# Three groups of transfers begun a stage earlier: the recurrence's first chunk, the first attention's first pair, the output weights' second half

## The chip, the cores and the metric

The kernel runs on one core of a Trainium2 chip. A core has a matrix engine (PE, its weight loads PEld), a vector engine (DVE), a scalar engine (ACT), GpSimd (POOL) and SyncE (SP), which here only issues transfers. All engines run their own instruction streams and meet through semaphores. All data is float32; the on-chip memory is one array named `arena` of 128 partitions by 53208 words. The metric is the device time of one execution in microseconds (us), median of three runs: 4931.64 us before the change (4931.13 to 4935.05).

## What is computed

Two blocks in a row, on 1024 tokens of width 1024. The first block:

```python
h = rmsnorm(x, g_mix_pre);  proj = h @ w_in
out_a = gated_deltanet(...)          # chunked delta rule, 4 heads of 128
out_b = dilated_attention(...)       # 8 heads of 64, with a bias table
x = x + rmsnorm(concat(out_a, out_b) @ w_out, g_mix_post)
x = x + rmsnorm((silu(h2 @ w_gate) * (h2 @ w_up)) @ w_down, g_ffn_post)
```

The second block has two layers, over the 1024 tokens and 256 context tokens:

```python
u = (x * (1 + scale) + shift) @ w_in
y_r = rwkv7_bidirectional(u)         # 6 heads of 64, forward and backward recurrence
y_a = grouped_query_attention(u)     # 6 query heads
y_n = neighbourhood_attention(u)     # 4 heads
x = layer_norm(ALPHA * x + gate * (concat(y_r * silu, y_a * silu, y_n * silu) @ w_out))
```

## The kernel before

The program is a list of stages. A stage has one generator per engine; `Stage.drive` steps the main stage's generator and those of the stages that run `beside` it (on another "lane", with semaphores of its own). At the end of a stage PE, ACT, DVE and POOL each count up `stage_end` (`arrive`) and wait until all four have (`leave`, the value `meet`). SP takes no part in that meeting: `emit` runs only the main stages' `sp` in order, so SP runs ahead until a wait that is written into `sp` stops it. Whatever stands behind such a wait in SP's stream waits too.

The order of the main stages is: token norm; `PairProj` (the projections of block 1, with the preparation of the delta rule beside it); `Gdn` (the delta rule); `Attention` (dilated, four pairs of heads, eight query tiles each); `TokenPairs` (product with `w_out`, with `TokenRows`, the normalization, beside it); `GatedPairs` and a second `TokenPairs` (the gated network); then for each of two layers `PairProj` (with `NaBand`, `RwkvPrep` and `GqaPrep` beside it, in this order), `Rwkv` (the recurrence, ten chunks), `Attention` `gqa` (three pairs, with `RwkvOut` beside it), `Attention` `na` (two pairs), and `TokenPairs`.

The matrix products of `PairProj` and `TokenPairs` use seven half-size products in place of eight (P1, P5, P6, P7, P2, P3, P4 in the order of issue, `ORDER`). Their operands are sums: T1 = B12 - B11, T2 = B22 - T1, T4 = B21 - T2, T3 = B22 - B12 for the right side, S1 to S4 for the left. DVE makes them at the start of `TokenPairs`, in the order S1, T1, S2, T2, T4, S4, T3, S3 (`right_sum` at L1086, `left_sum` at L1062). P1 needs B11, P5 needs T1, P6 needs T2 and P7 needs S3. B11 and B12 are rows 0 to 3 of the weights (transfers j = 0 to 3), B21 and B22 rows 4 to 7.

The waits of SP that matter here:

- `PairProj.sp` (L369): the stores of a unit's blocks at n = 5, 6, 7 (L380), before them the store of the context columns at n = 1 (L413). POOL waits at the end of the stage until all stores have landed (L595).
- `Rwkv.sp` (L3128): waits for `self.meet - 4`, the end of the stage ahead, then issues the ten transfers of chunk 0 (L3135), then the first two pairs of `gqa` (`next_loads`, L2385), then those of chunk 1. PE waits for the K, B, V and Q parts before its first product (L3218). On POOL the stage begins with two clears (L3163) and the table of decay factors `fc` (L3169 to L3172, 18 small products); the first thing DVE does with a product of PE is behind a wait for that table (L3386), and its result (L3394) is what POOL continues with (L3178, L3182).
- The first `Attention`: `first_loads` (L2387) waits for `gdn.meet` and then issues pair 0 (five transfers) and pair 1.
- `TokenPairs.sp` (L968): the dictionary `after` gives the stage's end to wait for ahead of transfer j. Block 1 has `{0: gdn.meet}`, so all eight rows of `w_out` are fetched during the attention. The layers of block 2 have `{0: gqa.meet, 4: na.meet}`: rows 4 to 7 wait for the end of `na`, because their place in `arena` (columns 4096 to 8191) holds the masks of `na`.

```python
dve.drain().then_inc(s.sem, 1)                # Rwkv.run_dve, L3385
dve.wait_ge(O.sem, O.at(0, "fc"))
for n in range(NCH + 1):
```

Of the kernel before, what the change touches and what calls it, by code (L numbers as in the profile page):

```python
# [12 lines left out]
P = 128  # L13
TOP = 53208
D = 1024
# [182 lines left out]
class Stage:  # L198
# [16 lines left out]
    def sp(self, sp): pass  # L215
# [47 lines left out]
class PairProj(Stage):  # L263
# [9 lines left out]
    def __init__(self, core, w, tiles, x, first, out, room, eighth=(), silu=(), late=(), keep=False):  # L273
# [58 lines left out]
        self.steps = (3 if self.alone else 0) + 8 * self.N  # L332
# [36 lines left out]
    def sp(self, sp):  # L369
# [33 lines left out]
        for u in range(self.N):  # L403
            for n in range(8):
                if n in (5, 6, 7):
                    store(u, ("22", "11", "12")[n - 5])
# [460 lines left out]
class TokenPairs(Stage):  # L867
# [6 lines left out]
    def __init__(self, core, room, w, lhs, first, n, sums=None, spare=None, after=()):  # L874
# [13 lines left out]
        if not sums:  # L888
            W = core.W.rearrange("p (k f) -> p k f", k=8)
            self.B = {f"B{i + 1}{j + 1}": W[:, 4 * i:4 * i + 4, 512 * j:512 * j + 512] for i in range(2) for j in range(2)}  # L890
# [77 lines left out]
    def sp(self, sp):  # L968
        E, C = self.s_pe, len(self.cuts)
        for j in range(self.chunks):  # L970
            if j in self.after:
                sp.wait_ge(self.c.stage_end.sem, self.after[j])
# [17 lines left out]
            else:  # L990
                sp.dma_start(self.c.W[:, j * D:j * D + D], self.w[j]).then_inc(self.c.w_in[j].sem, 16)
# [1284 lines left out]
class Attention(Stage):  # L2276
# [9 lines left out]
    def __init__(self, core, room, pairs, n_q, n_k, units, loads, out, bias=None, extra=(), pool_bias=None, once=(), gate=None,  # L2286
                 home=None, pair_room=None, extra_room=None, sems=(0, 1, 2), start=((), ()), ahead=False):
# [7 lines left out]
        pair = lambda *shape: (pair_room or room).take(core, *shape)  # L2295
# [8 lines left out]
        self.extra = [(extra_room or room).take(core, 2, n) for n in extra]  # L2304
# [18 lines left out]
        self.steps = self.N + 2  # L2323

# [718 lines left out]
def tri(a):  # L3043
    return a.rearrange("p (h t) -> p h t", h=3)
# [10 lines left out]
class Rwkv(Stage):  # L3055
# [4 lines left out]
    def __init__(self, core, rw, fac, y, areas):  # L3060
        super().__init__(core)
        self.rw, self.fac, self.y = rw, fac, y
# [14 lines left out]
        self.fc = core.region(areas[-1][1], NCH, 2 * RT)  # L3077
# [49 lines left out]

    def sp(self, sp):  # L3128
        E, A = self.s_pe, self.s_act

        def load(n, part, i):
            for d, c in ((0, n), (1, self.back(n))):
                for x in part:
                    src = self.rw[x + str(d) if x != "V" else "V"].rearrange("(j p) t -> p j t", p=P)[:, :, c * P:(c + 1) * P]
                    sp.dma_start(tri(self.b[f"{x}{d}{n % 2}"]), src).then_inc(self.c.w_in[3 * (n % 2) + i].sem, 16)  # L3135

        sp.wait_ge(self.c.stage_end.sem, self.meet - 4)
        load(0, "KBV", 0)
        load(0, "Q", 1)
        load(0, "R", 2)  # L3140
        self.next_loads(sp)
        for n in range(NCH + 1):
            if n + 1 < NCH:
                if n > 0:
                    sp.wait_ge(E.sem, E.at(0, f"tB1@{n - 1}"))
                load(n + 1, "KBV", 0)
                if n > 0:
                    sp.wait_ge(E.sem, E.at(0, f"G1@{n}"))
                load(n + 1, "Q", 1)
                if n > 0:  # L3150
                    sp.wait_ge(E.sem, E.at(0, f"O1@{n}"))
                load(n + 1, "R", 2)
# [604 lines left out]
def second_block(nc, core, a, p2, fac, ms, gate_rows, h, h_at, x_home):  # L3757
# [12 lines left out]
    for l in range(2):  # L3770
# [13 lines left out]
        rwkv = Rwkv(core, rw, fac, y_dir, [(h_at, h_at + KT * TOK2), (big, top - 64)])  # L3784
# [274 lines left out]
```

## Time and profile before

| | |
|---|---|
| median of three runs | 4931.64 us |
| the profiled execution | 4922.9 us, span 4921.1 us |
| mean granted clock of PE | 0.966 |
| PE busy | 4553.9 us (93%) |
| PEld busy | 2888.5 us (59%) |
| DVE busy | 2715.9 us (55%) |
| ACT busy | 1465.5 us (30%) |
| POOL busy | 975.7 us (20%) |

PE is busy nearly throughout, and matmuls are pipelined with modelled ends, so a busy PE isn't PE at its peak. The idle time that is left stands mainly at the seams of the stages. Every row of the trace begins with a start time counted from the span's start, so two rows of one stretch can be subtracted. "Releaser" is what ended an engine's idle time.

### The profile page before, as it was taken

To read this page: it belongs to the slowest core of one execution; us is meant where nothing else is said; L and a number is where in the kernel's file an instruction comes from. 1 tells how busy PE (TensorE), PEld (TensorE's weight loads), DVE (VectorE), ACT (ScalarE), POOL (GpSimd) and SP (SyncE) were. 2 spreads that over 40 slices of the span, in tenths; PEclk is the share of its full clock that TensorE was granted. 3 is DMA by queue.
4 is the path that set the end of the run, shared out by engine and by line. 5 is a ranking of instruction groups with operands and counts; after the bars stand their busy time and mean duration, and the time that the engine had idled before them with its cause. 6 is when DMAs were issued, how large, how long until landed. Compare 5 with 4: busy or idle time off the path is not lost. (4 is left out here: it accounts for less than half of the span.)

```text
span 4921.1 us, 96946 instructions
## 1 busy us (share of the span) xinstructions
PE 4553.9 (93%) x41054; PEld 2888.5 (59%) x41054; DVE 2715.9 (55%) x4643; ACT 1465.5 (30%) x2452; POOL 975.7 (20%) x1174
## 2 busy tenths in 40 slices
PE   7998978899999989998999888998999799989897
PEld 4445955444444445554999755654544499976563
DVE  3763457786432336765545466566686445436556
ACT  1222353200000113332223255533342133236552
POOL 0002311000100000001233233620000132324460
PEclk9999999999999999999999999999999899989998
DMA  2332022343424544444221112113444411111222
GB/s 91 112 98 74 2 82 82 124 135 114 162 94 160 177 134 150 143 162 134 64 61 55 46 45 56 50 61 120 150 146 163 138 55 55 54 32 52 72 56 76
DMA packets 344923, 471.84 MB, mean 96 GB/s; under 512 B 39799, under 2 KB 247959, under 8 KB 343536
## 3 DMA queue, kind: packets, MB, share of 16 engines
q1 hardware_dynamic: 292416, 267.83, 17.5%
q0 software_dynamic: 52080, 197.81, 11.5%
q8 instruction: 330, 5.41, 0.5%
q14 instruction: 97, 0.79, 0.1%
HBM read 330.50 MB, written 148.65 MB: 97 GB/s over the span
## 5 line engine op out<-in xcount | busy, mean ns | idle before, releaser
L471 PE MATMUL psum<-arena 128*128 128x512 f32 x2352 | 1035.4, 597 | 12.2 <-POOLq L222 6.5
L3212 PE MATMUL psum<-arena 64*64 64x64 f32 (+5 forms) x23040 | 905.1, 232 | 34.7 <-DMA arena<-rw_Q 23.9
L3212 PEld LDWEIGHTS psum<-arena 64*64 64x64 f32 (+3 forms) x23040 | 866.0, 144 | 75.7 <-issue 47.3
L471 PEld LDWEIGHTS psum<-arena 128*128 128x128 f32 x2352 | 448.1, 191 | 561.4 <-issue 542.1
L1028 PE MATMUL psum<-arena 128*128 128x512 f32 x1344 | 589.1, 599 | 21.8 <-DVE arena L1086 11.4
L686 PE MATMUL psum<-arena 128*128 128x512 f32 x1232 | 535.7, 595 | 6.2 <-DVE arena L752 2.7
L2585 DVE CUSTOM_DVE_ANT_0 arena<-psum,arena 128x512 f32<-128x512 f32 (+3 forms) x532 | 292.8, 588 | 326.3 <-PE psum L2472 309.1
L1028 PEld LDWEIGHTS psum<-arena 128*128 128x128 f32 x1344 | 257.0, 192 | 344.2 <-issue 321.3
L686 PEld LDWEIGHTS psum<-arena 128*128 128x128 f32 x1232 | 232.3, 190 | 302.9 <-issue 290.9
L2472 PE MATMUL psum<-arena 64*128 64x512 f32 (+3 forms) x1192 | 275.4, 548 | 105.3 <-DVE arena L2585 70.0
L3416 DVE TENSOR_TENSOR arena<-arena,psum 128x384 f32<-128x384 f32 x320 | 177.9, 556 | 330.8 <-PE psum L3212 297.4
L2550 ACT COPY arena<-psum 128x512 f32<-128x512 f32 (+3 forms) x532 | 244.3, 512 | 306.5 <-PE psum L2523 300.6
L2442 POOL TENSOR_TENSOR arena<-arena 128x512 f32<-128x512 f32 (+2 forms) x192 | 221.9, 1166 | 475.5 <-ACT arena L2550 475.3
L2523 PEld LDWEIGHTS psum<-arena 128*128 128x128 f32 x1736 | 186.6, 142 | 151.0 <-issue 118.0
L2556 ACT ACTIVATE arena<-arena 128x1280 f32<-128x1280 f32 (+5 forms) x244 | 256.8, 1066 | 46.2 <-DVEq L2606 46.1
L2523 PE MATMUL psum<-arena 128*128 128x128 f32 x1736 | 251.5, 283 | 10.5 <-ACT arena L2550 9.6
L2488 PE MATMUL psum<-arena 128*64 128x128 f32 x3472 | 251.1, 281 | 8.2 <-DVE arena L2600 8.2
L2488 PEld LDWEIGHTS psum<-arena 128*64 128x64 f32 x3472 | 187.0, 137 | 52.9 <-issue 34.4
L2472 PEld LDWEIGHTS psum<-arena 64*128 64x128 f32 x1192 | 100.5, 196 | 179.6 <-DVE arena L2585 100.8
L3372 ACT COPY arena<-psum 128x384 f32<-128x384 f32 x200 | 96.1, 480 | 321.6 <-PE psum L3212 321.6
L3192 POOL TENSOR_TENSOR arena<-arena 128x384 f32<-128x384 f32 x160 | 155.3, 997 | 171.9 <-PE psum L3212 171.9
L3376 ACT COPY arena<-psum 128x384 f32<-128x384 f32 x240 | 101.7, 496 | 204.2 <-PE psum L3212 203.7
(341 smaller groups left out, 5223.3 us busy)
## 6 DMA issues: line engine op xcount, KB each, us to landing
arena<-w_in SPq DMA_DIRECT2D x86, 512.0 KB, 5.7
proj<-arena SPq DMA_DIRECT2D x172, 256.0 KB, 2.0
arena<-w_mod POOLq DMA_DIRECT2D x24, 1024.0 KB, 5.7
arena<-proj POOLq DMA_DIRECT2D x34, 640.0 KB, 5.1
arena<-down_sum SPq DMA_DIRECT2D x40, 512.0 KB, 3.6
arena<-proj SPq DMA_DIRECT2D x28, 640.0 KB, 7.0
arena<-w_down SPq DMA_DIRECT2D x30, 512.0 KB, 3.6
x_home<-arena POOLq DMA_DIRECT2D x26, 512.0 KB, 4.2
```

The lines of the kernel that those rows point to most:

```text
L471: ins = pe.matmul(ps[:, b, :], L[:, k, :], R[:, k, :], start=(p in ("P1", "P5", "P6", "P7") and k == 0), stop=(k == KT // 2 - 1), skip_gro ...
L686: ins = pe.matmul(self.c.psum[:, b, :], L[:, k, :], R[:, k, :], start=(begins and k == 0), stop=(k == KT // 2 - 1), skip_group_check=True)
L1028: ins = pe.matmul(self.bank(j, b), self.left(p, j, left, *g)[:, k - g[0], :], R[:, k - k0, :], start=(x in ("P1", "P5", "P6", "P7") and k ...
L2442: ins = pool.tensor_tensor(t[:, 0:m], x[:, 0:m], x[:, 512:512 + m], ALU.add)
L2472: ins = pe.matmul(ps[:, j, at:at + m], self.q[HALF[j], self.slot(it), q * P:(q + 1) * P], self.k[HALF[j], self.slot(it), k0:k0 + m], start ...
L2488: pe.matmul(ps[HALF[j], bank, 0:P], self.vT[:, it % 2, tiles[c] * P + 64 * j:tiles[c] * P + 64 * j + 64], self.pt[n % 2][j][:, c * P:(c + ...
L2523: ins = pe.transpose(out[:, x:x + P], self.p[n % 3][j][:, at + x:at + x + P], ident)
L2550: act.copy(self.pt[n % 2][j][:, at:at + w], ps[:, 2 + j, 0:w]).then_inc(A.sem, 1)
L2556: act.activation(self.p[x][g][:, 0:wide], self.p[x][g][:, 0:wide], ACT.Exp, bias=low, scale=-1.0).then_inc(A.sem, 1)
L2585: dve.tensor_tensor_reduce(self.p[x][j][:, at:at + w], ps[:, j, 0:w], add, -1.0, 3e38, ALU.add, ALU.min, self.acc[:, 2 * x + j, g:g + 1]). ...
L3212: return pe.matmul(out, lhsT, rhs, start=first, stop=last, skip_group_check=not (first and last))
L3416: dve.tensor_tensor(dst, dst, ps, ALU.subtract).then_inc(s.sem, 1)
```

## The change

- `PairProj.sp` calls `next_loads` in its last unit, at n = 4, ahead of that unit's block stores. In block 2 that is the new `Rwkv.first_loads`: SP waits for the end of `RwkvPrep` (`prep.meet`) and issues chunk 0's ten transfers there. `Rwkv.sp` begins with `gqa`'s pairs instead. Chunk 0's ten buffers move to the top of the arena.
- The first `Attention` keeps the buffers of its pairs in two places far apart (`pair_at`): slot 0 in columns 2048 to 7167, which `Gdn` doesn't use, slot 1 in the old area. Pair 0 is fetched once `gemm.meet` has come, which is ahead of `Gdn`; pair 1 after `gdn.meet` as before.
- As slot 0 now lies where `w_out` goes, `TokenPairs` of block 1 fetches rows 0 and 1 after `gdn.meet` and rows 2 to 7 only after the last output of the attention's pair 2 (`out{3 * att.per - 1}`, counted by DVE).
- `TokenPairs` of block 2 has its rows 4 to 7 in the slot of `gqa`'s and `na`'s pair buffers that is free after `na`'s pair 0 (`low`), and fetches them after that pair's last output (`out{na.per - 1}`).

```diff
@@ PairProj
-        self.steps = (3 if self.alone else 0) + 8 * self.N
+        self.steps, self.next_loads = (3 if self.alone else 0) + 8 * self.N, lambda sp: None
...
         for u in range(self.N):
             for n in range(8):
+                if n == 4 and u == self.N - 1:
+                    self.next_loads(sp)
@@ TokenPairs
-    def __init__(self, core, room, w, lhs, first, n, sums=None, spare=None, after=()):
+    def __init__(self, core, room, w, lhs, first, n, sums=None, spare=None, low=None, after=()):
...
-            self.B = {f"B{i + 1}{j + 1}": W[:, 4 * i:4 * i + 4, 512 * j:512 * j + 512] for i in range(2) for j in range(2)}
+            W = [W[:, 0:4, :], W[:, 4:8, :] if low is None else low]
+            self.resident = [W[k // 4][:, k % 4, :] for k in range(8)]
+            self.B = {f"B{i + 1}{j + 1}": W[i][:, :, 512 * j:512 * j + 512] for i in range(2) for j in range(2)}
...
-                sp.wait_ge(self.c.stage_end.sem, self.after[j])
+                sp.wait_ge(*self.after[j])
...
-                sp.dma_start(self.c.W[:, j * D:j * D + D], self.w[j]).then_inc(self.c.w_in[j].sem, 16)
+                sp.dma_start(self.resident[j], self.w[j]).then_inc(self.c.w_in[j].sem, 16)
@@ Attention
-        pair = lambda *shape: (pair_room or room).take(core, *shape)
+        self.pair_at = pair_at and list(pair_at)
+        pair = lambda *shape: self.apart(*shape) if pair_at else (pair_room or room).take(core, *shape)
...
+    def apart(self, _, n):
+        at, far = self.pair_at
+        self.pair_at[0] += n
+        return self.c.arena[:, at:at + 2 * far].rearrange("p (a b) -> p a b", a=2)[:, :, 0:n]
@@ Rwkv
-        self.fc = core.region(areas[-1][1], NCH, 2 * RT)
+        self.fc = core.region(areas[0][1], NCH, 2 * RT)
...
+    def first_loads(self, sp):
+        sp.wait_ge(*self.ready)
+        for i, part in enumerate(("KBV", "Q", "R")):
+            self.load(sp, 0, part, i)
+
     def sp(self, sp):
         E, A = self.s_pe, self.s_act
...
         sp.wait_ge(self.c.stage_end.sem, self.meet - 4)
-        load(0, "KBV", 0)
-        load(0, "Q", 1)
-        load(0, "R", 2)
         self.next_loads(sp)
@@ second_block
-        rwkv = Rwkv(core, rw, fac, y_dir, [(h_at, h_at + KT * TOK2), (big, top - 64)])
+        rwkv = Rwkv(core, rw, fac, y_dir, [(top - 64 - 10 * 384, top - 64), (h_at, h_at + KT * TOK2), (big, top - 64 - 10 * 384)],
+                    (side.stage_end.sem, prep.meet))
+        gemm.next_loads = rwkv.first_loads
...
-                          after={0: gqa.meet, 4: na.meet})
+                          low=R(x_at, 4, 2 * TOK2)[:, :, TOK2:TOK2 + D],
+                          after={0: (core.stage_end.sem, gqa.meet), 4: (na.s_dve.sem, na.s_dve.at(0, f"out{na.per - 1}"))})
@@ program
-        room = Room((big, TOP))
+        room = Room((big + 5 * SEQ, TOP))
...
-                        sems=core.w_in[0:3], start=([(core.stage_end.sem, gdn.meet)], ()),
+                        sems=core.w_in[0:3], start=([(core.stage_end.sem, gemm.meet)], [(core.stage_end.sem, gdn.meet)]),
+                        pair_at=(2048, big - 2048),
...
-        prod = TokenPairs(core, room, [token(a["w_out"], k) for k in range(KT)], mixT, 0, SEQ // P, after={0: gdn.meet})
+        prod = TokenPairs(core, room, [token(a["w_out"], k) for k in range(KT)], mixT, 0, SEQ // P, after={0: (core.stage_end.sem, gdn.meet), 2: (att.s_dve.sem, att.s_dve.at(0, f"out{3 * att.per - 1}"))})
```

## Rows read from the trace of the kernel before

**Rows 1.** Who waited, PE alone: engine, line, releaser: us, times, longest.

```profile
PE psum L3212 <- DMA arena<-rw_Q: 23.9, 2, 12.0
...
PE psum L2472 <- DMA arena<-bias_band: 13.0, 1, 13.0
...
PE psum L1028 <- DVE arena L1086: 11.4, 2, 6.6
```

**Rows 2.** The chain that ended last: start us, us, what; last stage.

```profile
4790.61 9.96 DMA arena<-w_out
```

**Rows 3.** Timeline, delta rule to attention: start us, us, instruction [idle before].

```profile
620.30 0.10 POOL L2411 MEMSET arena<- 128x1 f32 x1 [15.49 <-ACTq L222]
...
632.55 0.80 PE L2472 MATMUL psum<-arena 64*128 64x128 f32 x4 [12.97 <-DMA arena<-bias_band]
...
635.34 3.04 PE L2240 MATMUL psum<-arena 128*128 128x512 f32 x4
```

**Rows 4.** Windows of 2 us: busy by engine, PEclk, DMA share, GB/s.

```profile
634.00:636.00 2.00, 1.82 (x5) 1.03 (x6) 0.59 (x5) 0.69 (x2) 0.00 (x0) 0.50 1.03 414
...
4402.00:4404.00 2.00, 2.00 (x5) 0.47 (x3) 0.00 (x0) 0.00 (x0) 0.00 (x0) 0.50 0.00 0
```

**Rows 5.** Timeline, first layer, projections to recurrence.

```profile
2318.36 0.37 SPq L3135 DMA_DIRECT2D arena<-rw_K  x1
...
2320.31 2.73 POOL L3172 TENSOR_TENSOR arena<-arena 128x3 f32<-128x3 f32 x18
...
2326.53 4.11 PE L3212 MATMUL psum<-arena 64*64 64x64 f32 x120 [11.84 <-DMA arena<-rw_Q]
...
2328.20 1.02 DVE L3394 TENSOR_TENSOR arena<-psum,arena 128x384 f32<-128x384 f32 x2 [8.94 <-PE psum L3212]
```

**Rows 6.** Timeline, second layer, the same place.

```profile
3898.09 2.74 POOL L3172 TENSOR_TENSOR arena<-arena 128x3 f32<-128x3 f32 x18
...
3904.51 3.64 PE L3212 MATMUL psum<-arena 64*64 64x64 f32 x120 [12.04 <-DMA arena<-rw_Q]
...
3906.18 1.02 DVE L3394 TENSOR_TENSOR arena<-psum,arena 128x384 f32<-128x384 f32 x2 [9.13 <-PE psum L3212]
```

**Rows 7.** Timeline, end of the projections: first layer, then one row of the second.

```profile
2174.15 1.07 POOL L3580 DMA_DIRECT2D arena<-proj  x2 [8.38 <-POOLq L222]
...
2283.79 0.80 SPq L413 DMA_DIRECT2D proj<-arena  x2
...
2292.40 3.22 POOL L3604 DMA_DIRECT2D kx<-arena  x6 [24.82 <-DVEq L3694]
...
2300.45 15.97 SPq L380 DMA_DIRECT2D proj<-arena  x4
...
2305.85 8.84 PE L471 MATMUL psum<-arena 128*128 128x512 f32 x16 [3.38 <-POOLq L222]
...
3870.29 3.23 POOL L3604 DMA_DIRECT2D kx<-arena  x6 [24.78 <-DVEq L3694]
```

**Rows 8.** Timeline, start of TokenPairs in block 1.

```profile
821.22 10.58 PE L1028 MATMUL psum<-arena 128*128 128x512 f32 x24 [1.46 <-DVEq L222]
...
832.83 9.68 PE L1028 MATMUL psum<-arena 128*128 128x512 f32 x22 [1.03 <-DVE arena L1062]
...
836.54 0.69 DVE L1092 TENSOR_TENSOR arena<-arena,psum 128x512 f32<-128x512 f32 x1 [0.71 <-PE psum L1028]
```

**Rows 9.** Timeline, start of TokenPairs in the second layer.

```profile
4789.27 7.14 PE L1028 MATMUL psum<-arena 128*128 128x512 f32 x16 [1.91 <-DVEq L222]
...
4800.69 4.62 DVE L1086 TENSOR_TENSOR arena<-arena 128x2048 f32<-128x2048 f32 x2 [7.89 <-DMA arena<-w_out]
...
4812.95 0.69 DVE L1092 TENSOR_TENSOR arena<-arena,psum 128x512 f32<-128x512 f32 x1 [0.48 <-PE psum L1028]
```

**Rows 10.** Timeline, start of TokenPairs in the first layer.

```profile
3245.26 7.87 PE L1028 MATMUL psum<-arena 128*128 128x512 f32 x14
...
3267.47 0.69 DVE L1092 TENSOR_TENSOR arena<-arena,psum 128x512 f32<-128x512 f32 x1 [0.66 <-PE psum L1028]
```

More of the change, by code:

```diff
@@ L2286, in __init__ @@
     def __init__(self, core, room, pairs, n_q, n_k, units, loads, out, bias=None, extra=(), pool_bias=None, once=(), gate=None,
-                 home=None, pair_room=None, extra_room=None, sems=(0, 1, 2), start=((), ()), ahead=False):
+                 home=None, pair_room=None, pair_at=None, extra_room=None, sems=(0, 1, 2), start=((), ()), ahead=False):
         super().__init__(core)
@@ L2303, in __init__ @@
         self.rec, self.acc, self.nm, self.zero = take(2, P), take(6, 4), take(6, 1), take(1)
-        self.extra = [(extra_room or room).take(core, 2, n) for n in extra]
+        self.extra = [pair(2, n) if pair_at else (extra_room or room).take(core, 2, n) for n in extra]
         self.tree = [[take(min(self.width - 512, 512)) for _ in range(2)] for _ in range(2)]
@@ L3055, with __init__ @@
 class Rwkv(Stage):
-    def __init__(self, core, rw, fac, y, areas):
+    def __init__(self, core, rw, fac, y, areas, ready):
         super().__init__(core)
-        self.rw, self.fac, self.y = rw, fac, y
+        self.rw, self.fac, self.y, self.ready = rw, fac, y, ready
         self.nb = 8
@@ L3126, in back, with load @@
         return nctx - 1 - n if n < nctx else NCH + nctx - 1 - n
+    def load(self, sp, n, part, i):
+        for d, c in ((0, n), (1, self.back(n))):
+            for x in part:
+                src = self.rw[x + str(d) if x != "V" else "V"].rearrange("(j p) t -> p j t", p=P)[:, :, c * P:(c + 1) * P]
+                sp.dma_start(tri(self.b[f"{x}{d}{n % 2}"]), src).then_inc(self.c.w_in[3 * (n % 2) + i].sem, 16)
+    def first_loads(self, sp):
+        sp.wait_ge(*self.ready)
+        for i, part in enumerate(("KBV", "Q", "R")):
+            self.load(sp, 0, part, i)
     def sp(self, sp):
         E, A = self.s_pe, self.s_act
[L3131 to L3135, printed above, removed]
         sp.wait_ge(self.c.stage_end.sem, self.meet - 4)
-        load(0, "KBV", 0)
-        load(0, "Q", 1)
-        load(0, "R", 2)
         self.next_loads(sp)
@@ L3145, in sp @@
                     sp.wait_ge(E.sem, E.at(0, f"tB1@{n - 1}"))
-                load(n + 1, "KBV", 0)
+                self.load(sp, n + 1, "KBV", 0)
                 if n > 0:
                     sp.wait_ge(E.sem, E.at(0, f"G1@{n}"))
-                load(n + 1, "Q", 1)
+                self.load(sp, n + 1, "Q", 1)
                 if n > 0:
                     sp.wait_ge(E.sem, E.at(0, f"O1@{n}"))
-                load(n + 1, "R", 2)
+                self.load(sp, n + 1, "R", 2)
             if n > 0:
@@ L3971, in program @@
         room = Room((big + FFT * SEQ, TOP))
-        prod = TokenPairs(core, room, kview(a["w_down"]), act, 0, SEQ // P, sums, h[:, :, TOK2 - 512:TOK2], after={6: ffn.meet})
+        prod = TokenPairs(core, room, kview(a["w_down"]), act, 0, SEQ // P, sums, h[:, :, TOK2 - 512:TOK2], after={6: (core.stage_end.sem, ffn.meet)})
         prod.beside = [TokenRows(core.lanes[1], room, prod, tiles, "rms", {"g": row_of(a["rows"], 1)}, h, extra=extra, slots=1)]
```

## The prediction

> **What bounds the kernel now.** I read the waits of PE first, since PE is busy 93% of the span. Three of its waits are for a transfer that begins only when the stage that needs it begins: 23.9 us in two pieces before the recurrence (one per layer), 13.0 us before the first attention, and 11.4 us in two pieces inside `TokenPairs`, where the row names DVE's sum (L1086) as the releaser [rows 1]. The chain that ended last goes through the third kind: 9.96 us of `w_out` a few microseconds after the last stage opens [rows 2]. Then I read the timeline of each of these five seams, and asked not how long PE waits but what would be late next, since DVE and POOL have start-up work of their own in the same microseconds. In all five the stage order is a barrier for every computing engine, so a microsecond saved at a seam shifts all that follows.
>
> **The change part by part.** Everything is taken from the profiled execution (4922.9 us); the median is 8.7 us above it, and I carry the saving over to the median unchanged.
>
> *First attention.* POOL's first instruction of the stage is at 620.30, PE's first product at 632.55, and PE had been idle for 12.97 us, that is since 619.58 [rows 3]. With pair 0 fetched ahead of the delta rule, PE can start about 0.1 us after the stage opens, at 620.4. DVE and POOL only clear small tiles there (0.10 us). The saving is 632.55 - 620.4 = 12.15 us. Pair 1 still leaves at 620.3; it is needed eight query tiles later. The first tiles are short chains PE, DVE, ACT, and between them PE waits as it did. The clock is the unknown. After the idle 12.97 us PE ran at the granted clock 0.50, the 1.2 GHz level [rows 4], and the product beside the attention took 3.04 us [rows 3]. If the new start, which comes after only 0.8 us of idle, keeps 2.4 GHz, up to half of that and of the small products around it goes, 2 us. Against that, in the second layer's `gqa` start, a sparse start that followed a busy stage with a short gap, the clock stood at 0.50 even 14 us in [rows 4]; if the same happens here for such a time, with PE busy about two thirds of it, it costs some 3 us. I take 0, nearer to neither, and keep -3 to +2. Part: **12.1 us**.
>
> *The recurrence, twice.* PE waits until 2326.53, and SP issues the first transfer at 2318.36, which is when the stage opens [rows 5]. The whole wait would be 8.1 us. But DVE may not touch PE's first product before POOL has made the table of decay factors, and this ends at 2320.31 + 2.73 = 2323.04 [rows 5]. Now DVE's first product is at 2328.20; with the data present it comes at about 2323.1, 5.1 us earlier. From there POOL's and PE's chain (L3178, L3182, PE) follows as now. In the second layer the table ends at 3898.09 + 2.74 = 3900.83 and DVE's product was at 3906.18 [rows 6]: 5.3 us. So PE's wait shrinks by 8 us, but PE gets a new wait of some 3 us a moment later, behind its first 120 products; what ends last is POOL's table. Part: **10.4 us**, bounds 9 (PE at the low clock for longer, since its work there is now broken in two) and 11.7 (DVE no longer waits 0.7 us between its two kinds of first products, as ACT has then long delivered).
>
> *What the moved issue costs.* The ten transfers go ahead of the last unit's block stores on SP's queue. SP has issued the context store at 2283.79 + 0.80 and its next instruction is a block store that could not leave before 2300.45 [rows 7]. Ten issues of about half a microsecond each fit in this hole: no store is later. The wait for `RwkvPrep` ahead of them passes at once: POOL began `GqaPrep`, which comes behind that meeting, at 2174.15 [rows 7]. In the old place the ten transfers took from 2318.36 to 2326.53, 8.2 us in all [rows 5]; from 2284.6 that ends at about 2292.8. POOL's six stores of `kx` leave from 2292.40, and PE waits for their landing (through the end of `GqaPrep`) until 2305.85, 3.38 us [rows 7]. The overlap is under a microsecond. I cost it at nothing. In the second layer `kx` leaves at 3870.29 [rows 7] and the last unit has no context store ahead of the hole, so SP is there earlier still. The first two pairs of `gqa` and chunk 1 leave 5 us earlier than now and are needed tens of microseconds later: nothing.
>
> Here a rule of the Trainium skill speaks against the change (DMA: Bandwidth & Descriptors, "Issuing engines are not separate DMA queues"): transfers issued by SP and by GpSimd run on the same 16 engines and interleave, so an early load isn't free for a store on another queue. By the rule, with the two bursts on top of each other, the stores of `kx` would be late by as much as the loads take; by the rows they nearly miss each other. This is the second rival below.
>
> *TokenPairs in block 2, twice.* Block 1's stage is the pattern, since all its weights are present: it starts at 821.22, three products take 10.58 us, P7 starts at 832.83, 11.6 us after the start, because DVE's sums (S3 is the last) take this long; DVE's sum after P7 is at 836.54, 15.3 us after the start [rows 8]. In the second layer the stage starts at 4789.27, T2 waits 7.89 us for `w_out`, and the sum after P7 is at 4812.95, 23.7 us after the start [rows 9]. With rows 4 to 7 present this stage should run as block 1's: 23.7 - 15.3 = 8.4 us. That is more than the DMA wait, for two reasons: P6 ran at the low clock after the gap, and PE's gap was longer than what DVE lost. In the first layer PE's first two products end at 3245.26 + 7.87 = 3253.13 and the sum after P7 is at 3267.47 [rows 10]. P6 adds a third of 10.58, 3.5 us, so 3256.7; S3 is ready at about 3255.9, so it isn't the limit; P7 and its sum take 836.54 - 832.83 = 3.7 us more [rows 8]: 3260.4, and the saving is 7.1 us. Part: **15.5 us**. The bound from below is PE's gap alone, 11.4 us [rows 1]; from above 16.5, had the first layer its early products at the second's pace. SP's new wait here is for `na`'s pair 0, half a stage before the end; four rows take about 10 us [rows 2], and behind it in SP's queue stand only the next stage's loads, which wait for PE's last product anyway.
>
> *w_out in block 1* now comes after the attention's pair 2, a quarter of the 200 us stage (620.30 to 821.22 [rows 3, 8]) before it is needed: 50 us for six rows, which at the pace of [rows 2] take 15 us. Nothing; without that cover it would cost what block 2's stages lost.
>
> **Sum:** 12.1 + 10.4 + 15.5 = 38.0 us, so 4922.9 becomes 4884.9 in a profiled execution and the median 4931.6 becomes **4893.6**. With all bounds at their ends the saving is 29.5 or 44 us: 4902 or 4887.5.
>
> **The rivals.**
> *The clock takes part of it back.* PE has less idle time at the seams, but the starts stay sparse, and PE stays at 1.2 GHz longer in the attention and in both recurrences. For it: the row at 4402 [rows 4]. Against it: in `TokenPairs` the opposite must happen, as dense products follow on each other. Price 3 us and twice 2 us: 4900 us. Chance 0.15.
> *The loads collide with the stores of `kx`.* If the ten loads push the landing of `kx` by their full 8.2 us, PE's wait of 3.38 us at L471 grows by this in both layers [rows 5, 7]: 16.4 us lost, 4910 us. Against it: the loads start 7.8 us before. Chance 0.06.
> *It doesn't do what it says in the first attention:* PE waits for something else at 620.4, or pair 1 lands too late for tile 8 and the wait comes back there. That gives 12.1 us back: 4906 us. Against it: tile 8 comes over 20 us later. Chance 0.04.
> *Slower than before.* SP now waits for `RwkvPrep` ahead of the last unit's stores, and the stage can't end before these land. One microsecond that `RwkvPrep` ends after 2300.45 is one microsecond that the stage ends later. Below about 19 us per layer the rest of the saving still covers it; from there the kernel is slower, and at 25 us late per layer it would be 4944 us. In the trace `RwkvPrep` ended over 120 us before [rows 7], so the change would have to slow it greatly, which nothing in it does. Chance 0.02.
>
> **How the numbers follow.** The forecast has 0.73: 4893.6, its own range 4888 to 4900. Adding the clock's rival and half of the others' nearer side, and the 1 to 3 us by which medians of this kernel move, the range is 4886 to 4905. A measurement of this kernel can tell about 0.2%, 10 us, from no change; a saving below 10 us needs the collision and another failure together. Faster 0.96, same 0.02, slower 0.02.
>
> **What would show each step.** Right: `rw_Q` and `bias_band` are gone from PE's waits; DVE L3394 comes 4.8 us after the recurrence's stage opens, straight after POOL L3172, and PE shows a new wait for POOL L3182 of 3 to 4 us; the sum after P7 comes 15 to 16 us after each `TokenPairs` starts, and no DMA wait stands at L1086; PE's wait at L471 for POOL's queue stays at 3 to 4 us. Wrong: a wait at L471 of over 5 us (collision); the first 15 us of the attention at the low clock; stores of the last unit issued later than 2300; a wait for `w_out` at the start of block 1's `TokenPairs`.

## The result, and the profile after

In the first series of timings the changed kernel took 4878.42 us (median of four, 4876.26 to 4880.86) and the kernel before 4931.39 us (4928.27 to 4935.05): a ratio of 0.9892, 95% interval 0.9875 to 0.991, a saving of 53 us (by the interval 44 to 62) where 38.0 us was forecast. The forecast said 4893.6 us with a range of 4886 to 4905, so the direction was right and the size wrong. Two further series, taken with the experiments, gave smaller savings:

| series | before, median (runs) | changed, median (runs) | saving | ratio, 95% interval |
|---|---|---|---|---|
| first | 4931.39 (4) | 4878.42 (4) | 53.0 | 0.9892, 0.9875 to 0.991 |
| second | 4926.11 (7) | 4882.45 (4) | 43.7 | 0.9913, 0.9898 to 0.9927 |
| third | 4927.76 (9) | 4880.19 (4) | 47.6 | 0.9902, 0.9886 to 0.9918 |
| all executions | 4927.7 (35) | 4880.9 (13) | 46.8 | |

The 35 executions of the kernel before lie between 4917 and 4939 us (standard deviation 4.9), the 13 of the changed one between 4876 and 4886 (3.1). So there are two questions: what the five openings really gave, and what the rest is.

The head of the changed kernel's page: the span, and the busy time of the engines.

```profile
span 4875.0 us, 96946 instructions
PE 4541.5 (93%) x41054; PEld 2881.5 (59%) x41054; DVE 2716.3 (56%) x4643; ACT 1465.8 (30%) x2452; POOL 976.6 (20%) x1174
```

Who waited on PE, changed kernel (engine, line, releaser: us in total, times, longest):

```profile
PE psum L3226 <- POOL arena L3196: 9.9, 4, 4.4
...
PE psum L3226 <- POOLq L222: 7.7, 2, 4.0
PE psum L473 <- POOLq L222: 7.1, 2, 4.1
...
PE psum L1033 <- DVEq L222: 5.3, 3, 1.9
...
PE psum L1033 <- DVE arena L1067: 3.1, 3, 1.0
```

All three waits of [rows 1] are gone: no transfer of `rw_Q` or `bias_band` releases PE, and in `TokenPairs` DVE's sum costs 3.1 us for three stages, the waits that block 1's stage always had. A new wait stands at the top, PE for POOL's L3196 in the recurrence (L3182 before), as the forecast said.

**First attention.** The timeline of PE, changed kernel (start us, us, instruction, idle before and its releaser), which answers [rows 3], and two windows (length, busy time of PE, PEld, DVE, ACT, POOL, then the granted clock, the share of DMA and GB/s), which answer [rows 4]:

```profile
615.75 0.50 PE L1960 MATMUL psum<-arena 128*128 128x128 f32 x3
616.96 0.49 PE L2484 MATMUL psum<-arena 64*128 64x128 f32 x4 [0.71 <-ACTq L222]
618.30 0.70 PE L2484 MATMUL psum<-arena 64*128 64x256 f32 x4 [0.84 <-DVEq L2618]
618.93 1.98 PE L2245 MATMUL psum<-arena 128*128 128x512 f32 x4
```

```profile
615.00:620.00 5.00, 3.44 (x23) 2.28 (x22) 2.49 (x13) 2.34 (x4) 1.25 (x3) 1.00 0.40 121
620.00:625.00 5.00, 4.33 (x22) 2.00 (x21) 1.04 (x4) 3.83 (x8) 0.00 (x0) 1.00 1.01 406
```

PE starts 0.71 us after the delta rule's last product instead of 12.97 us, and the granted clock stays at 1.00 (2.4 GHz) through the opening, while pair 1 keeps the DMA engines full behind it. So the same four instructions take 0.49 us for 0.80, 0.70 for 1.23 and 1.98 for 3.04 [rows 3].

**Recurrence.** The timeline of its opening in the first layer and DVE's and POOL's rows of the second, changed kernel, against [rows 5, 6]:

```profile
2299.04 3.23 PE L3226 MATMUL psum<-arena 64*64 64x64 f32 x120 [3.71 <-POOLq L222]
2299.09 1.41 POOL L3177 MEMSET arena<- 128x768 f32 x2 [23.50 <-POOLq L222]
...
2300.96 2.74 POOL L3186 TENSOR_TENSOR arena<-arena 128x3 f32<-128x3 f32 x18
...
2303.73 1.02 DVE L3408 TENSOR_TENSOR arena<-psum,arena 128x384 f32<-128x384 f32 x2 [3.82 <-POOL arena L3186]
2304.37 0.99 POOL L3192 TENSOR_TENSOR arena<-arena 128x384 f32<-128x384 f32 x1 [0.67 <-DVE arena L3408]
...
2306.68 1.54 PE L3226 MATMUL psum<-arena 64*64 64x64 f32 x24 [4.41 <-POOL arena L3196]
...
3869.47 1.41 POOL L3177 MEMSET arena<- 128x768 f32 x2 [22.97 <-POOLq L222]
...
3874.12 1.02 DVE L3408 TENSOR_TENSOR arena<-psum,arena 128x384 f32<-128x384 f32 x2 [3.82 <-POOL arena L3186]
```

PE begins with the stage, but DVE sits 3.82 us behind POOL's table and starts 4.64 us after POOL's clear in the first layer and 4.65 us in the second. Before, it was 2328.20 - 2318.44 = 9.76 and 3906.18 - 3896.22 = 9.96 us (POOL's clear began at 2318.44 and 3896.22). The openings save 5.1 and 5.3 us, the forecast's two numbers.

**TokenPairs in block 2.** The openings in both layers, changed kernel, against [rows 8 to 10]:

```profile
3226.80 10.58 PE L1033 MATMUL psum<-arena 128*128 128x512 f32 x24 [1.91 <-DVEq L222]
...
3238.41 4.96 PE L1033 MATMUL psum<-arena 128*128 128x512 f32 x11 [1.03 <-DVE arena L1067]
...
3242.12 0.69 DVE L1097 TENSOR_TENSOR arena<-arena,psum 128x512 f32<-128x512 f32 x1 [1.06 <-PE psum L1033]
...
4751.92 10.58 PE L1033 MATMUL psum<-arena 128*128 128x512 f32 x24 [1.91 <-DVEq L222]
...
4767.25 0.69 DVE L1097 TENSOR_TENSOR arena<-arena,psum 128x512 f32<-128x512 f32 x1 [1.06 <-PE psum L1033]
```

The sum after P7 comes 15.32 and 15.33 us after the opening, as in block 1's stage [rows 8]. (In two of the changed kernel's four profiles the first layer has 15.7.) In the second layer it was 23.68 us before [rows 9]: 8.35 saved.

**Queues.** The end of the projections, changed kernel, against [rows 7]:

```profile
2264.59 0.45 SPq L3144 DMA_DIRECT2D arena<-rw_K  x1
...
2272.36 3.23 POOL L3618 DMA_DIRECT2D kx<-arena  x6 [24.82 <-DVEq L3708]
...
2286.54 8.79 PE L473 MATMUL psum<-arena 128*128 128x512 f32 x16 [4.12 <-POOLq L222]
```

The loads start 7.8 us ahead of `kx`, as reckoned from the rows of before. PE's wait behind `kx` is 4.12 us for 3.38, and in the second layer 2.94. The first profile of the kernel before had a short one: from POOL's first store of `kx` to PE's product it takes 13.45 to 14.22 us there in five profiles of the first layer (mean 13.9), and 14.0 to 14.2 in the changed kernel's four. In the second layer both have 13.5 in the mean. So the moved loads cost the stores 0.2 us at most.

### The profile page after: what moved, and what is told of

Its sections match the earlier page's. It is cut to its first block and busy times, and to the rows that moved or that the text cites. A ratio compares the mean times of both kernels' runs of the same rounds, so it can differ in the third digit from the quotient of the medians.

```text
span 4875.0 us, 96946 instructions
## 1 busy us (share of the span) xinstructions
PE 4541.5 (93%) x41054; PEld 2881.5 (59%) x41054; DVE 2716.3 (56%) x4643; ACT 1465.8 (30%) x2452; POOL 976.6 (20%) x1174
## 5 line engine op out<-in xcount | busy, mean ns | idle before, releaser
L473 PE MATMUL psum<-arena 128*128 128x512 f32 x2352 | 1034.1, 596 | 14.0 <-POOLq L222 7.1
L473 PEld LDWEIGHTS psum<-arena 128*128 128x128 f32 x2352 | 446.9, 191 | 562.8 <-issue 543.2
```

Source lines behind the costliest of these rows:

```text
L473: ins = pe.matmul(ps[:, b, :], L[:, k, :], R[:, k, :], start=(p in ("P1", "P5", "P6", "P7") and k == 0), stop=(k == KT // 2 - 1), skip_gro ...
```

## The experiments

All run the whole computation. Lines in the diffs are against the changed kernel unless said otherwise. To find where time went, I took the start of the same vector, scalar and GpSimd instructions in two profiles and followed how their distance grows from stretch to stretch; "the openings" are the stretches around the five seams.

**One part at a time** (e1 to e3), against a saving that may sit elsewhere. The recurrence's part alone (e1_rec), the attention's part alone (e2_att) and the output weights' part of block 2 alone (e3_low) are the changed kernel with the two others undone. The lines that undo `TokenPairs`' part (in e1 and e2), the attention's (in e1 and e3) and the recurrence's (in e2 and e3):

```
-                          low=R(x_at, 4, 2 * TOK2)[:, :, TOK2:TOK2 + D],
-                          after={0: (core.stage_end.sem, gqa.meet), 4: (na.s_dve.sem, na.s_dve.at(0, f"out{na.per - 1}"))})
+                          after={0: (core.stage_end.sem, gqa.meet), 4: (core.stage_end.sem, na.meet)})
...
-                        sems=core.w_in[0:3], start=([(core.stage_end.sem, gemm.meet)], [(core.stage_end.sem, gdn.meet)]),
-                        pair_at=(2048, big - 2048),
+                        sems=core.w_in[0:3], start=([(core.stage_end.sem, gdn.meet)], ()),
...
+        for i, part in enumerate(("KBV", "Q", "R")):
+            self.load(sp, 0, part, i)
         self.next_loads(sp)
...
-        gemm.next_loads = rwkv.first_loads
```

> The kernel before with one part of the change: the recurrence's first chunk is fetched behind the last unit's products, the rest is as before. Theory of the seams (what is saved is what the five stage openings save, and the openings do not act on each other): DVE's first product comes 5.1 to 5.8 us earlier after the opening in the first layer and 5.3 to 5.5 us in the second, nothing before or behind them moves, and the time is 10 to 12 us below the kernel before. Theory of the clock elsewhere (part of the change's 53 us is a granted clock that is higher in stretches away from the seams, whichever part brings it): over 14 us below, with the surplus at the recurrence's sparse ends. Rival that the last state step pays it back (in the full change that step of the first layer ran at clock 0.50 and lost 8 us): 2 to 4 us below.

> The kernel before with one part of the change: the first attention's pair 0 and its bias band are fetched beside the delta rule, and rows 2 to 7 of block 1's output weights wait for the attention's pair 2. Theory of the seams: 12 to 14 us below the kernel before; 12.1 if the clock after the opening is as it was (0.50 for the first products), 14 if PE keeps clock 1.00 through the opening and its first products are shorter, which the trace of the full change shows (first product beside the attention 1.98 us for 3.04). Theory of the clock elsewhere: over 16 us below, with the surplus in the delta rule ahead of the seam or in the attention's later tiles.

> The kernel before with one part of the change: in block 2's TokenPairs the last four rows of the output weights have a place of their own and are fetched half a stage ahead. Theory of the seams: the sum after P7 comes 15 to 16 us after the opening in both layers, 7.1 to 7.9 and 8.4 us earlier than in the kernel before, and the time is 15 to 17 us below it. Theory of the clock elsewhere: over 20 us below, since dense products from the opening on keep PE at clock 1.00 in what follows. If only PE's gap goes and DVE's sums end last: 11 us below.

> The kernel before, unchanged, for a second profile of it. Theory of the seams with a scatter of the clock: its profiled span is not the 4922 us of the first profile but nearer to the 4931 us median, and what it has more stands in stretches with sparse products (the delta rule, the last state steps of the recurrences, the state-space scans) at a lower granted clock, up to 8 us in a stretch. Theory of a gain elsewhere through the change: its span is 4920 to 4925 us and every stretch away from the seams agrees with the first profile within 1 us.

Measured in one series, the kernel before at 4928.75 us (9 runs):

| part | median (5 runs) | saving, ratio and interval | openings in its profile | forecast |
|---|---|---|---|---|
| e1_rec | 4910.68 | 18.1; 0.9962, 0.9949 to 0.9974 | 9.76 - 4.64 and 9.96 - 4.65: 10.4 | 10.4 |
| e2_att | 4909.82 | 18.9; 0.9966, 0.9954 to 0.9979 | 14.1, and 0.7 behind it | 12.1 |
| e3_low | 4910.56 | 18.2; 0.9966, 0.9952 to 0.9979 | 7.85 + 8.36: 16.2 | 15.5 |

The parts add: 55 us by medians, 41 by openings, as the whole gives 53 and 41. The openings came out as expected. The medians all came out above, but they share one median of the kernel before, and by their intervals the savings are 13 to 25, 10 to 23 and 10 to 24 us: for e2 and e3 the openings' sum lies inside, for e1 it does not. The second profile of the kernel before (e4_before, 4929.0 us) shows why profiles alone can mislead: it is 6.1 us longer than the first, and as much stands in one place, the last state steps of the first layer's recurrence, which hold the same instructions. Here they are in the first profile of the kernel before:

```profile
2787.54 4.38 PE L3212 MATMUL psum<-arena 64*128 64x64 f32 x48 [1.56 <-ACT arena L3376]
2792.26 2.89 PE L3212 MATMUL psum<-arena 128*128 128x64 f32 x24 [0.35 <-ACT arena L3376]
```

and in the second:

```profile
2787.76 11.56 PE L3212 MATMUL psum<-arena 64*128 64x64 f32 x72 [1.60 <-ACT arena L3376]
```

The 72 products take 7.3 us at granted clock 1.00; here, with the clock falling to 0.50 among them, 11.56 us. My forecast was made from the profile that had the short ones, and was carried to medians that hold a mixture.

**Is the surplus steady?** Three profiles of the changed kernel more (e6, e8, e12), one of the kernel before (e7), and then, since e1 had gained 18 us where its openings give 10, two more of e1 (e13, e14) and of before (e15, e16).

> The changed kernel, unchanged, in five more rounds and a second profile. Theory of the seams with a scatter of the clock: 4876 to 4884 us; its profile agrees with the first of the changed kernel within 1 us at every seam, and differs by 5 to 8 us at the last state steps of the recurrences, each of which is either at the low clock or not. Theory of a steady gain at the recurrences' ends: the last state step of the second layer keeps clock 1.00 again as in the first profile (it was at 0.50 in both profiles of the kernel before and in the one without the recurrence's part, e3_low).

> The kernel before, unchanged, a third profile. Scatter of the clock: the last state step of each layer's recurrence is at the low clock or not, anew for each (first profile: not, yes; second: yes, yes). Steady difference: yes in the second layer again, and the span is then 4920 to 4928 us.

> The changed kernel, unchanged, a third profile. Scatter of the clock: the last state step of each layer is at the low clock or not, anew. Steady gain: not in the second layer again.

> The changed kernel, unchanged, third series. If the five openings are all that the change saves: 40 to 44 us below the kernel before, as in the second series (43.7) and by the rows of the seams (41.8), not 53 us as in the first. If something steady is gained besides: 48 us or more.

> The kernel before with the recurrence's part alone, a second profile. Steady gain at the recurrences' ends: as in its first profile the end of the first layer's recurrence is as in the first profile of the kernel before (within 1 us) and the second layer's 5 to 6 us shorter; 4907 to 4912 us. Chance: either of them may come out 4 to 8 us otherwise; 4906 to 4920 us. The openings save 3.5 to 5.5 us each in both cases.

> The same once more, a third profile, with the same expectations: steady if both ends are again as in the first, chance if not.

> The kernel before, a fourth profile. In three so far the end of the first layer's recurrence was 0, 6.1 and 4.4 us longer than in the first profile, and the second layer's 0, 0.3 and 2.5 us shorter. Steady: the second layer's within 0 to 2.5 us again. Chance: 5 to 6 us shorter in one of the two.

> The kernel before, a fifth profile, with the same expectations as the fourth.

What the end of each recurrence gained against the first profile of the kernel before, in us (start of the same vector instructions after it, less that ahead of it; in the second layer the stretch takes in the first 25 us of `gqa`):

| | first layer | second layer | span |
|---|---|---|---|
| before, five profiles | 0, -6.1, -4.4, -7.6, -5.9 | 0, +0.3, +2.5, +9.7, +4.1 | 4921.1, 4927.2, 4925.9, 4925.6, 4921.4 |
| e1_rec, three | -0.1, -5.7, -5.7 | +5.8, +2.5, +2.5 | 4906.9, 4914.1, 4915.0 |
| changed, four | -7.5, -5.8, -7.5, -5.9 | +5.7, -0.8, +9.7, +5.8 | 4875.0, 4884.5, 4883.9, 4879.8 |

The rows of PE in the second layer, fourth profile of the kernel before (e15), where the clock stayed up:

```profile
4379.23 4.38 PE L3212 MATMUL psum<-arena 64*128 64x64 f32 x48 [1.57 <-ACT arena L3376]
4383.96 2.89 PE L3212 MATMUL psum<-arena 128*128 128x64 f32 x24 [0.35 <-ACT arena L3376]
```

and in the second profile (e4), where it didn't:

```profile
4372.13 12.09 PE L3212 MATMUL psum<-arena 64*128 64x64 f32 x72 [1.57 <-ACT arena L3376]
```

The theory of a steady gain falls: with the kernel unchanged the second layer's end came out 9.7 us shorter once (5.7 in the state steps, the rest in `gqa`'s first tiles) and not at all another time, and e1's ends did not repeat. e2_att, which leaves the recurrence as it was, has -5.8 and +5.7. Which execution gets which is chance as far as these profiles go. A shift of the odds is not excluded: in the second layer the 72 products were short in three of the changed kernel's four profiles and in one of five before. (The Trainium skill, TensorE: Matmul & The Clock Gate, Part 1, says that the same kernel shows different numbers of slow products from run to run; the traces agree, as in the second layer of the unchanged kernel these products took 7.3 us in one profile and 11.3 to 12.8 in four.)

The runs of e13 and e14 were 4915.97 and 4916.87 us, 5 to 6 us over the median of e1's first five and inside the range expected for chance (4906 to 4920), not in that for a steady gain (4907 to 4912). The third series (e12) gave 47.6 us, between the two expectations (40 to 44, or 48 and more), and decides nothing. By the mean of the profiles the change saves 4924.2 - 4880.8 = 43.4 us. Of this 42.3 stand in the stretches around the five openings (15.1, 5.0, 8.1, 5.5 and 8.6); the two recurrence ends have -1.9 and +1.8, and all other stretches together about 1. By the medians of all executions the change saves 46.8 us.

**PE's gap and the clock** (e9_band). Of pair 0 only q, k and v come early; the two bias transfers leave when the stage opens:

```
-        self.load(sp, 0)
+        late = 2 if self.pair_at else 0
+        for dst, src in self.loads[0][:len(self.loads[0]) - late]:
+            sp.dma_start(dst, src).then_inc(self.sems[0].sem, 16)
+        if late:
+            for sem, value in self.start[1]:
+                sp.wait_ge(sem, value)
+            for dst, src in self.loads[0][3:]:
+                sp.dma_start(dst, src).then_inc(self.sems[0].sem, 16)
```

> The changed kernel, but of the first attention's pair 0 only q, k and v come ahead of the delta rule; its two bias transfers (2 of the 5) leave when the attention's stage opens, ahead of pair 1. It asks how PE's gap at this seam and the granted clock behind it hang together. My reading: the seam (end of the delta rule's last product group to the second product of the output norm) was 24.0 us before and is 9.86 us in all three profiles of the change; 12.2 us of the 14.1 are the wait and the other 2 are products that no longer run at 0.50. With two transfers left PE should wait 4 to 6 us; if the clock falls over such a gap, the seam is 9.9 + 5 + up to 2 = 15 to 17 us and the first product beside the attention takes 3.04 us again; if it doesn't fall, 14 to 15 us with that product at 1.98 us. Rival, the bias is not what is needed first: PE waits under 1 us and the seam stays at 9.9 us. The time is 4 to 7 us over the changed kernel's, by the rival equal.

Timeline of PE, and two windows, of this kernel:

```profile
622.94 0.80 PE L2491 MATMUL psum<-arena 64*128 64x128 f32 x4 [5.55 <-DMA arena<-bias_band]
```

```profile
620.00:625.00 5.00, 1.23 (x6) 1.00 (x8) 0.51 (x4) 0.45 (x2) 0.00 (x0) 0.66 0.99 383
625.00:630.00 5.00, 5.00 (x18) 2.36 (x18) 0.78 (x4) 1.19 (x3) 0.00 (x0) 0.66 1.02 401
```

From the end of the delta rule's last products to the second product of the output norm the changed kernel takes 9.86 us in each of its four profiles (9.85 once), this kernel 16.83 (15 to 17 expected) and the kernel before 24.00, 23.72, 23.95, 25.78 and 25.62. The wait grew by 5.55 - 0.71 = 4.8 us, the seam by 7.0: the other 2.1 us are products at the low clock (the first of the norm took 3.30 us for 1.98). Here a gap of 5.55 us cost the clock, one of 0.71 us didn't. The median was 4886.38 (4 runs, 4878.1 to 4902.3), 6.2 us over the changed kernel in its series; the runs scatter too much to add to that.

The row of `gqa`'s start in the second layer that the prediction set against this [rows 4] has a gap of its own ahead of it. PE's first product there, kernel before, and two windows around it:

```profile
4388.80 2.08 PE L2472 MATMUL psum<-arena 64*128 64x512 f32 x4 [2.77 <-POOLq L222]
```

```profile
4386.00:4388.00 2.00, 0.04 (x2) 0.00 (x0) 0.00 (x0) 0.48 (x1) 0.00 (x0) 1.00 0.21 65
...
4390.00:4392.00 2.00, 0.88 (x4) 0.00 (x0) 0.96 (x3) 0.00 (x0) 2.00 (x5) 0.50 0.53 166
```

PE was idle for 2.77 us, and the clock went from 1.00 to 0.50 at its end. So that row stood for a gap about four times the 0.71 us that the changed attention has.

**The collision with `kx`, brought about by a wait** (e10_kx):

```
         sp.wait_ge(*self.ready)
+        sp.wait_ge(*self.beside_kx)
...
+        k_dve = gemm.beside[2].s_dve
+        rwkv.beside_kx = (k_dve.sem, k_dve.at(3, "out"))
         gemm.next_loads = rwkv.first_loads
```

> The changed kernel, but SP waits for the same vector product as POOL's six stores of kx before it issues the recurrence's ten first loads, so that the loads (8.2 us alone) run beside the stores in both layers: the collision of my second rival made on purpose. If transfers issued by the two engines share what moves them and the stores are short of it: PE's wait for POOL at the projections' last product grows from 3 to 4 us to 7 to 12 us in each layer, and the time is 8 to 16 us over the changed kernel's. If the stores are bound by something of their own: that wait stays within 1 us and only a late landing of the chunk can cost, at most 3 us per layer; within 4 us in all.

Timeline of the end of the projections, first layer, then PE's product in the second:

```profile
2274.13 0.37 SPq L3144 DMA_DIRECT2D arena<-rw_K  x1
2274.34 3.23 POOL L3619 DMA_DIRECT2D kx<-arena  x6 [24.82 <-DVEq L3709]
...
2280.04 4.64 SPq L3144 DMA_DIRECT2D arena<-rw_Q  x2
...
2284.73 2.35 SPq L3144 DMA_DIRECT2D arena<-rw_R  x2
...
2289.02 8.54 PE L473 MATMUL psum<-arena 128*128 128x512 f32 x16 [4.62 <-POOLq L222]
...
3863.16 9.94 PE L473 MATMUL psum<-arena 128*128 128x512 f32 x16 [4.09 <-POOLq L222]
```

A window of 10 us that starts 2.7 us after POOL's first store, in the changed kernel and then in this one:

```profile
2275.00:2285.00 10.00, 7.16 (x17) 2.94 (x16) 2.07 (x3) 1.23 (x2) 0.59 (x2) 1.00 0.86 217
```

```profile
2277.00:2287.00 10.00, 7.14 (x17) 2.94 (x16) 2.07 (x3) 1.23 (x2) 0.56 (x2) 1.00 1.00 276
```

SP's ten issues took 13 us (2274.13 to 2287.08), in the changed kernel 5.3 (2264.59 to 2269.86). Yet PE's wait at L473 was only 4.6 and 4.1 us. From POOL's first store to PE's product it took 14.7 and 14.4 us, against 14.15 and 13.5 in the mean of the changed kernel's four profiles: 0.5 and 0.9 us more, with 8.2 us of loads on top of the stores. The windows suggest why it is so little, though no run tests it. Without the loads the stores (and the block stores behind them) show a share of 0.86 at 217 GB/s, with the loads 1.00 at 276, and at the attention's opening above a share of 1.01 goes with 406 GB/s: a share near 1 doesn't say that no more can be moved.

Against the changed kernel's profile of the same series (e12) the second layer's opening lost 2.8 us; 0.8 of them is this wait (4.09 us for 3.25) and 1.2 PE's last product behind it, which ran longer at the low clock (9.94 us for 8.71). The median was 4888.79 us, 8.6 over the changed kernel; 3.4 of that are at the two openings (0.6 and 2.8) by the profiles, the rest in no place that the change of this kernel explains. For the wait the second expectation was right in the first layer (within 1 us) and nearly in the second; the 7 to 12 us of the first expectation came in neither layer, and the 8.6 us of the whole fit the first by number only. (The rule of the Trainium skill, DMA: Bandwidth & Descriptors, "Issuing engines are not separate DMA queues", that the transfers of both engines run on the same DMA engines and interleave, agrees with SP's stretched issues, 13 us for 5.3. What I made of it in time was several times too high, because I let the stores wait for the whole burst of loads.)

**POOL's table** (e5_table, and e11_table2 in another series). The table is computed behind POOL's work on chunk 0, and DVE waits for it in chunk 1:

```
-        dve.wait_ge(O.sem, O.at(0, "fc"))
...
                         dve.wait_ge(s.sem, s.at(0, f"H@{n}"))
+                        if n == 1:
+                            dve.wait_ge(O.sem, O.at(0, "fc"))
```

> The changed kernel, with POOL's table of decay factors computed behind POOL's products of chunk 0 instead of ahead of them, and DVE waiting for it at its first use in chunk 1. If the table is what ends last at the recurrence's opening, as my forecast's step says: POOL's first product with the identity comes 2.7 us earlier after each opening, and the time is 4 to 6 us below the changed kernel's. Rival, PE's own start ends last (loads of weights and the first 120 products at the low clock): DVE's first product comes at most 1 us earlier and the time is within 2 us of the changed kernel's, since ACT and PE are then the limit.

> The changed kernel with POOL's table behind chunk 0, again, to set it against the changed kernel in one series. By its first profile each recurrence begins 2.5 to 2.7 us earlier than in the changed kernel: 5 us below it. If that is given back within the recurrence's tail, where the granted clock falls: 0 to 2 us below.

Timeline of the opening, first layer, e5:

```profile
2302.78 4.10 PE L3228 MATMUL psum<-arena 64*64 64x64 f32 x120 [3.71 <-POOLq L222]
2302.83 1.42 POOL L3178 MEMSET arena<- 128x768 f32 x2 [23.41 <-POOLq L222]
...
2304.38 1.02 DVE L3409 TENSOR_TENSOR arena<-psum,arena 128x384 f32<-128x384 f32 x2 [0.73 <-PE psum L3228]
...
2305.03 0.99 POOL L3184 TENSOR_TENSOR arena<-arena 128x384 f32<-128x384 f32 x1 [0.79 <-DVE arena L3409]
```

DVE now starts 1.55 us after POOL's clear (0.95 us in the second layer) for 4.64, released by PE. Against the first profile of the kernel before, the changed kernel gains 4.1 and 5.1 us around the openings (mean of four profiles) and this one 6.95 and 7.5 (mean of two): another 2.8 and 2.3 us. So the table did end last there. By medians the kernel is 5.4 us faster than the changed one (4877.09 to 4882.45) and 3.8 us in the other series (4876.36 to 4880.19); its nine runs scatter from 4864.7 to 4886.6, so the saving of 5 us is shown at its place and only likely in the total. Its ratios to the kernel before are 0.9907 (0.989 to 0.9923) and 0.9895 (0.9877 to 0.9914).

## Why the prediction was off

| term | forecast | first pair of profiles | means of five profiles before and four changed |
|---|---|---|---|
| first attention | 12.1 | 24.00 - 9.86 = 14.1 | 24.6 - 9.86 = 14.8 |
| recurrence, first layer | 5.1 | 9.76 - 4.64 = 5.1 | 9.88 - 4.65 = 5.2 |
| recurrence, second layer | 5.3 | 9.96 - 4.65 = 5.3 | 9.70 - 4.65 = 5.1 |
| TokenPairs, first layer | 7.1 | 23.18 - 15.32 = 7.9 | 23.65 - 15.5 = 8.1 |
| TokenPairs, second layer | 8.4 | 23.68 - 15.33 = 8.35 | 23.94 - 15.33 = 8.6 |
| sum | 38.0 | 40.7 | 41.8 |

The mechanism was right: what was waited for at the five openings, and, but for `TokenPairs` in the first layer, what ends last there once the transfers are early. Two terms of the sum were too small, and the step from the sum to a measured median was the larger part of the miss, about 5 us of it unexplained.

*First attention: mis-sized by 2 us.* The step that failed is "I take 0, nearer to neither" for the clock. The rows for both ends were there, but the one taken for a loss (the sparse start of `gqa`) stands behind an idle time of 2.77 us, at the end of which the clock fell. Here PE was dense until 0.71 us before the start, and the clock stayed at 1.00 in all changed profiles. The end +2 was the right value (14.1 measured for 12.1), and e9 shows it from the other side.

*Recurrence: right,* in the numbers and in what ends last: POOL's table in both layers, a new wait of 4.4 us on PE (3 to 4 forecast), and the time back when the table is moved.

*TokenPairs, second layer: right. First layer: 0.8 us short.* I worked from the end of the first two products, 3253.13, and added 3.5 us for P6. But these products had themselves run partly at the low clock (they end 8.8 us after the opening at 3244.29; at full clock two thirds of 10.58, 7.1 us). With the weights present they run at full clock, and DVE's S3 is the limit as in block 1. The pattern alone, 15.3 us after the opening, would have given 7.9.

*The costs taken at nothing were nothing or nearly.* The moved issue fell into the hole of SP's queue; PE's wait at L473 is 0.7 us longer in one layer and 0.2 shorter in the other in the first pair of profiles, by the means 0.2 us and nothing; nothing waits for `w_out` in block 1's `TokenPairs`, nor for pair 1. *Of the rivals,* the clock's had the wrong sign at the attention, and the collision's price was several times too high: with the bursts fully on top of each other (e10) the stores cost PE 0.5 and 0.9 us, not 8.2. The loads found room beside the stores (276 GB/s for 217).

*The total.* Of the 15 us between 38.0 and the first series' 53.0, the openings explain 2.7 to 3.8. Another 6.2 is that series against all executions (53.0 to 46.8). The step that failed here is the widening by "the 1 to 3 us by which medians of this kernel move": I read it from three runs that agreed within 4 us, while 35 runs have a standard deviation of 4.9 us, and profiles show single stretches that move by 6 to 10 us. From these scatters I estimate a standard deviation of some 3 us for a difference of two medians of four, and the range should have had twice that on both sides. Its lower end would then have been near 4882, still above the 4878.4 us of the first series and the 4880.9 of all executions. The base was uncertain in the same way: 4931.6 is 3.9 us above the median of 35. Set against all executions, 4927.7 - 38.0 = 4889.7 and the changed kernel's 4880.9 us differ by 8.8 us, still more than the mis-sized terms, which take 3.8 of them. A slip besides: the bounds that the prediction adds up to a saving of 44 us (14.1 + 11.7 + 16.5) give 42.3.

*What stays open:* about 5 us between the openings (41 to 42) and the medians (46.8). Were all executions independent, their scatter would put the saving between 44 and 49 us, so chance alone is an uneasy answer; but they come from several series that differ among themselves by 9 us. The mean of the profiles has 43.4, and no stretch away from the openings shows a gain that repeats. Whether the rest is chance, short state steps that come more often, or many small gains in clock, these runs can't tell.

## What to carry to other kernels

When a wait in front of a stage is removed, read what will be late next (here a 2.7 us table on POOL) and compute from the pattern of a stage that already has its data; those two readings gave three of five terms within 0.1 us, and what ends last in three of the four seams of block 2. When you take the granted clock at a seam from another row, compare how long PE was idle ahead of both: 0.71, 2.77, 5.55 and 12.97 us here are not one case. The idle time alone doesn't settle it either, since the clock also fell among the products of the last state step, in 24 of the 36 that 18 profiles hold, where PE had been idle for only 1.6 us. And take the scatter of a kernel from more than three runs, or from two profiles laid side by side, before a range is written.

## What the runs showed of the hardware

- After 12.97, 5.55 and 2.77 us without a product PE came back at granted clock 0.50, that is 1.2 GHz; after 0.71 us it stayed at 2.4 GHz in all four profiles of the changed kernel.
- The same 72 products of the last state step take 7.3 us or 11.1 to 13.0 us, in 18 profiles of this kernel and its variants and in both layers, by whether the clock falls when they come.
- Ten loads on SP's queue (8.2 us alone) begun together with six stores on POOL's raised the DMA share from 0.86 to 1.00 and the rate from 217 to 276 GB/s over 10 us, and PE's product that waits for the stores came only 0.5 and 0.9 us later; SP's issues stretched from 5.3 to 13 us.
